# Two heads at a time in the last eight attention steps of block 2's last mixer

## What is computed

```python
def odd_mixer(hn, w_in, qn, kn, w_out):
    z = (hn @ w_in).reshape(B, S, 3, 16, 64)
    q, k, v = rms_norm(z[:, :, 0], qn), rms_norm(z[:, :, 1], kn), z[:, :, 2]
    o = moba_attention(q, k, v, alibi_slopes(16), 64 ** -0.5)
    return o.reshape(B, S, 1024) @ w_out
# 256 tokens are one block of keys, so moba_attention is causal attention:
#   scores = q k^T - slope * distance, masked; softmax; times v
```

## Time and profile before

| | us |
|---|---|
| median of three runs | 1979.36 |
| lowest, highest | 1979.27, 1981.42 |
| the profiled execution itself | 1981.44 |
| its span | 1979.70 |

### The profile page before, as it was taken

The page is one execution under the profiler, slowest core; times in us unless marked ns, Lnnn a source line. Parts: engine busy times, 40 slices in busy tenths (PEclk is TensorE's granted clock), DMA queues, the critical chain, the costliest instruction groups (busy, mean ns, idle before and its releaser), DMA issues.

```text
span 1979.7 us, 24390 instructions
## 1 busy us (share of the span) xinstructions
PE 1946.0 (98%) x9160; PEld 1594.2 (81%) x9160; DVE 1211.2 (61%) x1506; ACT 919.5 (46%) x1143; POOL 85.0 (4%) x161
## 2 busy tenths in 40 slices
PE   9999999999999999999999999899999999999999
PEld 7888888887888788788878888786788887778887
DVE  5555776677446644667668555676555466765545
ACT  5443435545443444343653544366444355644433
POOL 2000100000000100000000000000000000000000
PEclk9999999999999999999999999998999999999999
DMA  9575653446554855564445655453365555336542
GB/s 311 189 220 177 214 189 130 168 149 213 191 191 149 270 190 185 191 219 160 140 169 167 216 184 184 135 173 124 118 239 170 170 180 182 107 123 233 171 168 86
DMA packets 201325, 353.51 MB, mean 179 GB/s; under 512 B 7985, under 2 KB 101089, under 8 KB 201249
## 3 DMA queue, kind: packets, MB, share of 16 engines
q1 hardware_dynamic: 195856, 334.85, 50.7%
q0 software_dynamic: 5392, 17.62, 2.9%
HBM read 351.39 MB, written 1.05 MB: 178 GB/s over the span
## 4 chain that ended last, share of the span: by engine, by line
PE 85%; DVE 5%; issue 5%; DVEq 2%; ACT 2%; DMA 0%; POOL 0%; SPq 0%; ACTq 0%; POOLq 0%
PE acc L686 48%; PE aux L686 29%; DVE w_low L2050 1%; PE aux L802 1%; PE aux L701 1%; PE aux L956 1%; ACT w_high L1492 1%; DVE x_res L2136 1%; PE aux L1250 1%; DVE xT_low L2056 0%; PE aux L1249 0%; DVEq L2102 0%; PE aux L1270 0%; PE aux L1258 0%; DMA w_raw<-ffn_w 0%
## 5 line engine op out<-in xcount | busy, mean ns | idle before, releaser
L2050 DVE TENSOR_TENSOR w_low<-w_raw,w_high 128x2048 fp32r<-128x2048 f32 (+2 forms) x308 | 695.5, 2271 | 425.8 <-ACT w_high L1492 423.3
L1492 ACT CAST w_high<-w_raw 128x2048 fp32r<-128x2048 f32 (+1 forms) x312 | 587.6, 1898 | 431.2 <-PE acc L686 323.9
L686 PE MATMUL aux<-w_high,xT_high 128*128 128x512 f32 x960 | 380.8, 397 | 3.5 <-DVE xT_low L2056 1.7
L686 PE MATMUL aux<-w_high,xT_low 128*128 128x512 f32 x960 | 374.7, 390 | 0.0
L686 PE MATMUL aux<-w_low,xT_high 128*128 128x512 f32 x960 | 373.8, 389 | 0.0
L686 PE MATMUL acc<-w_high,yT_high 128*128 128x512 f32 (+1 forms) x836 | 330.9, 396 | 2.4 <-DVE yT_low L2202 2.3
L686 PE MATMUL acc<-w_high,yT_low 128*128 128x512 f32 (+1 forms) x836 | 326.0, 390 | 0.0
L686 PE MATMUL acc<-w_low,yT_high 128*128 128x512 f32 (+1 forms) x836 | 325.8, 390 | 0.0
L686 PE MATMUL acc<-w_high,xT_high 128*128 128x512 f32 (+2 forms) x752 | 297.4, 395 | 5.7 <-DVE xT_low L2056 4.1
L686 PE MATMUL acc<-w_high,xT_low 128*128 128x512 f32 (+2 forms) x752 | 291.5, 388 | 0.0
L686 PE MATMUL acc<-w_low,xT_high 128*128 128x512 f32 (+2 forms) x752 | 291.2, 387 | 0.0
(11 more groups left out here) (307 smaller groups left out, 1356.5 us busy)
## 6 DMA issues: line engine op xcount, KB each, us to landing
w_raw<-ffn_w SPq DMA_DIRECT2D x174, 512.0 KB
w_raw<-w_ff SPq DMA_DIRECT2D x64, 1024.0 KB
w_raw<-w_in SPq DMA_DIRECT2D x52, 1024.0 KB
w_raw<-ffn_w SPq DMA_DIRECT2D x44, 1024.0 KB
w_raw<-w_branch SPq DMA_DIRECT2D x16, 1024.0 KB
w_raw<-o_w_in SPq DMA_DIRECT2D x12, 1024.0 KB
w_raw<-w_ple_gate SPq DMA_DIRECT2D x8, 1024.0 KB
w_raw<-e_w_in SPq DMA_DIRECT2D x6, 1024.0 KB
```

Source lines behind the costliest of these rows:

```text
L686: last = nc.tensor.matmul(dst, lhs[:, kt, tok], rhs(j), start=(kt == k_first and q == 0), stop=(kt == k_last and q == 2))
L1492: nc.scalar.copy(whi[:, s, 0:size], raw[:, s, 0:size]).then_inc(slot_hi[s], 1)
L2050: V.tensor_tensor(wlo[:, s, 0:size], raw[:, s, 0:size], cast(whi[:, s, 0:size]), ALU.subtract)\
```

## The change

The steps of heads 0 to 7 stay as they are, but for the values of head 6, which move out of step 7, and for two jobs of ScalarE in step 7 that change places (the copy of head 7 now comes ahead of the copy of z5). Heads 8 to 15 are done in four iterations g = 4 to 7 of two heads. TensorE's order in one: values of pair g-1, scores of heads 2g+2 and 2g+3, six products, transposes of 2g, three products, transposes of 2g+1, three products (in g = 4 the six products come first). The last pair's values stand in `out_end`.

- `score_pair` interleaves two heads: both short matmuls, then both long ones. The heads lie on different row halves. It waits until both banks are read.
- `values_pair` interleaves two heads on the two column halves of `woven_o`.
- ScalarE's order in an iteration: copy of pair g-1, copies of heads 2g and 2g+1, exponentials of 2g+2 and 2g+3, a high unit in g = 4, 5 and 6.
- VectorE keeps its order head by head; only the low part of a pair moves, from odd steps to even ones (from h = 8 on, pair h/2-1 ahead of the scores of h+2).
- There are four buffers of probabilities in place of three; the turned probabilities of odd heads go to another buffer.

The same products are computed, from the same weight units.

```diff
@@ -370,18 +370,18 @@
-            return stat_[:, :, :].rearrange("p a b -> p (a b)")[:, 2 * (h % 3) + t:2 * (h % 3) + t + 1]
+            return stat_[:, :, :].rearrange("p a b -> p (a b)")[:, 2 * (h % 4) + t:2 * (h % 4) + t + 1]
...
-            return stat_[:, :, :].rearrange("p a b -> p (a b)")[:, 2 * (h % 3):2 * (h % 3) + 2]
+            return stat_[:, :, :].rearrange("p a b -> p (a b)")[:, 2 * (h % 4):2 * (h % 4) + 2]
...
         def probs(h):
-            return flat(bk)[:, (h % 3) * 3 * P:(h % 3 + 1) * 3 * P]
+            return flat(bk)[:, (h % 4) * 3 * P:(h % 4 + 1) * 3 * P]
...
         def probs_T(h):
-            return flat(bk)[:, (3 + h % 2) * 3 * P:(4 + h % 2) * 3 * P]
+            return aT if h % 2 else flat(bk)[:, 4 * 3 * P:5 * 3 * P]
@@ -1195,7 +1195,7 @@
             quad2("c", xTh, xTl, tile1=norm_T1, tile1_at=(1, 0))
-            def piece(name, j, t):
+            def piece(name, j, t, ks=range(4)):
@@ -1205,9 +1205,9 @@
                 vh, vl = (w[:, s, :].rearrange("p (k n) -> p k n", k=4) for w in (whi, wlo))
-                last = products(acc[:, p, t, :], [(4 * j + k, k) for k in range(4)], 0, KT - 1, xTh, xTl, t,
+                last = products(acc[:, p, t, :], [(4 * j + k, k) for k in ks], 0, KT - 1, xTh, xTl, t,
                                 lambda k: vh[:, k, :], lambda k: vl[:, k, :])
-                if (j, t) == (1, 1):
+                if (j, t, ks[-1]) == (1, 1, 3):
                     last.then_inc(acc_full[p], 1)
@@ -1238,6 +1238,19 @@
+            def score_pair(n0, h, q, k, late=()):
+                if h >= 2:
+                    pe.wait_ge(s_ready, DEPTH * H1 + n0 + h)
+                for name in late:
+                    p, n = JOB[name]["acc"][0]
+                    pe.wait_ge(acc_read[p], acc_n2(p, n) + 2)
+                for i in (h, h + 1):
+                    nc.tensor.matmul(woven_score(i)[:, 0:P], q(i, 0, P), k(i, 0, P), start=True, stop=True)
+                for i in (h, h + 1):
+                    nc.tensor.matmul(woven_score(i)[:, P:3 * P], q(i, P, S), k(i, 0, S), start=True, stop=True)\
+                        .then_inc(score_full, 1)
             def score(n0, h, q, k, late=()):
@@ -1258,6 +1271,19 @@
                 at_T[n0 + h] = n_aux[2].k + 1
+            def values_pair(n0, g, v):
+                pe.wait_ge(aux_read[2], at_T[n0 + 2 * g + 1])
+                if g > 0:
+                    pe.wait_ge(o_read, n0 // 2 + g)
+                heads = [(woven_o[i * HD:(i + 1) * HD, :], probs_T(i), v(2 * g + i)) for i in range(2)]
+                for o, p, (v0, v1) in heads:
+                    nc.tensor.matmul(o[:, 0:P], v0, p[:, 0:P], start=True, stop=True)
+                for o, p, (v0, v1) in heads:
+                    nc.tensor.matmul(o[:, P:S], v0, p[:, P:2 * P], start=True, stop=False)
+                for o, p, (v0, v1) in heads:
+                    nc.tensor.matmul(o[:, P:S], v1, p[:, 2 * P:3 * P], start=False, stop=True).then_inc(o_full, 1)
@@ -1387,6 +1413,10 @@
+            def odd_scores(h):
+                score_pair(ODD0, h, lambda h, c0, c1: half(flat(bv), h, c0, c1),
+                           lambda h, c0, c1: half(kT_odd, h, c0, c1))
             def odd_v(h):
@@ -1401,8 +1431,8 @@
             odd_score(1)
-            for h in range(MOBA_H):
-                if h + 2 < MOBA_H and h not in (0, 6):
+            for h in range(8):
+                if h not in (0, 6):
                     odd_score(h + 2)
@@ -1425,28 +1455,42 @@
                     odd_score(8)
-                elif h == 7:
+                else:
                     piece("z5", 1, 1)
-                elif h == 8:
+                probs_turned(ODD0, h)
+                if 0 < h < 7:
+                    values(ODD0, h - 1, odd_v)
+            for g in range(4, MOBA_H // 2):
+                if g == 4:
                     out_piece("oout", 0, 0, (0, 1))
-                elif h == 9:
-                    out_piece("oout", 1, 0, (0, 1))
-                elif h == 10:
-                    out_piece("oout", 0, 0, (2, 3))
-                elif h == 11:
+                values_pair(ODD0, g - 1, odd_v)
+                if 2 * g + 2 < MOBA_H:
+                    odd_scores(2 * g + 2)
+                if g == 5:
+                    out_piece("oout", 0, 1, (0, 1))
+                elif g == 6:
                     out_piece("oout", 1, 0, (2, 3))
-                elif h == 12:
-                    out_piece("oout", 0, 1, (0, 1))
-                elif h == 13:
-                    out_piece("oout", 0, 1, (2, 3)).then_inc(unit_used, 1)
-                elif h == 14:
+                elif g == 7:
                     out_piece("oout", 2, 0, (0, 1))
+                probs_turned(ODD0, 2 * g)
+                if g == 4:
+                    out_piece("oout", 1, 0, (0,))
+                elif g == 5:
+                    out_piece("oout", 0, 0, (2,))
+                elif g == 6:
+                    out_piece("oout", 0, 1, (2,))
                 else:
-                    out_piece("oout", 3, 0, (0, 1))
-                probs_turned(ODD0, h)
-                if h > 0:
-                    values(ODD0, h - 1, odd_v)
-            out_end("oout", lambda: values(ODD0, MOBA_H - 1, odd_v))
+                    out_piece("oout", 3, 0, (0,))
+                probs_turned(ODD0, 2 * g + 1)
+                if g == 4:
+                    out_piece("oout", 1, 0, (1,))
+                elif g == 5:
+                    out_piece("oout", 0, 0, (3,))
+                elif g == 6:
+                    out_piece("oout", 0, 1, (3,)).then_inc(unit_used, 1)
+                else:
+                    out_piece("oout", 3, 0, (1,))
+            out_end("oout", lambda: values_pair(ODD0, MOBA_H // 2 - 1, odd_v))
             ff_and_side(1)
@@ -1952,7 +1996,7 @@
                 nc.scalar.copy(probs_T(h), aux[:, 2, 0:3 * P]).then_inc(aux_read[2], 1)
-                if h % 2 == 0 and h > 0:
+                if h % 2 == 0 and h > 0 and n0 == 0:
                     pair_copy(n0, h // 2 - 1)
@@ -2008,11 +2052,10 @@
             head_exps(ODD0, 1, 1.0)
-            for h in range(MOBA_H):
+            for h in range(MOBA_H // 2):
                 if h == 6:
                     copy_T("kt1", kT_odd[:, D:2 * D], 2)
-                if h + 2 < MOBA_H:
-                    head_exps(ODD0, h + 2, 1.0)
+                head_exps(ODD0, h + 2, 1.0)
                 if h == 1:
@@ -2021,17 +2064,26 @@
                     nc.scalar.copy(two(buf[:, D:2 * D]), acc[:, 0]).then_inc(acc_read[0], 1)
-                elif h == 7:
+                head_copies(ODD0, h)
+                if h % 2 == 0 and h > 0:
+                    pair_copy(ODD0, h // 2 - 1)
+                if h == 7:
                     full("z5")
                     to_sbuf("z5", bval[:, :, NC:D])
-                head_copies(ODD0, h)
                 if h < 3:
...
                     high_unit(unit0 + 8 + h)
-                elif h in (8, 9):
-                    high_unit(unit0 + h + 6)
-                elif h == 13:
+            for g in range(4, MOBA_H // 2):
+                pair_copy(ODD0, g - 1)
+                head_copies(ODD0, 2 * g)
+                head_copies(ODD0, 2 * g + 1)
+                for h in (2 * g + 2, 2 * g + 3):
+                    if h < MOBA_H:
+                        head_exps(ODD0, h, 1.0)
+                if g in (4, 5):
+                    high_unit(unit0 + 10 + g)
+                elif g == 6:
                     split_unit("oout", 0)
@@ -2893,8 +2945,10 @@
             for h in range(MOBA_H):
-                if h % 2 and h > 1:
+                if h in (3, 5, 7):
                     pair_low((h - 3) // 2)
+                elif h % 2 == 0 and h > 7:
+                    pair_low(h // 2 - 1)
                 if h + 2 < MOBA_H:
...
```

## The result

Over 20 executions each, the changed kernel takes 1983.51 us in the median (1979.21 to 1986.37) and the kernel before 1979.65 us (1977.51 to 1984.56). The ratio, an estimate from the executions of both kernels (it is not the quotient of the medians, which lie 3.86 us apart), is 1.0014 with a 95% interval of 1.0008 to 1.0020: 2.8 us slower, 1.6 to 4.0. The forecast was 1981.2 us, slower by 1.85, and a range of 1977.5 to 1986.5. One of the 12 executions of experiment e1 took 2159.01 us at a mean granted clock of 0.85 and is left out of its ratio. The profiled execution took 1983.08 us with a span of 1981.3 us, against 1981.44 and 1979.7: 1.6 us more.

The account below looks back on a forecast made before the run. TensorE, busy 98%, was taken to bound the kernel; 6.8 us leave it, but 9.5 us of waits on a VectorE and ScalarE loop come (0.8 were there): 1979.36 + 1.85 = 1981.2 us, range 1977.5 to 1986.5.

Parts of the forecast that it names:

- the walk: Three engine queues followed in written order from head 7's transposes: 9.5 us of waits come, last values 1.8 us later.
- TensorE's own queue: Heads 8 to 15: scores in pairs 2.5, values in pairs 4.0, products in quarters 0.3, together 6.8 us less.
- rival C: Value pairs: column halves do not overlap, 1.46 us a pair, 3.2 us slower in all, 1982.5 us; chance 0.10.
- The loop: VectorE and ScalarE jobs from probabilities(2g+1) round to the next probabilities set the pace, 8.8 us a pair, no TensorE job.
- Weight loads at nothing: Low units 14 and 15 end 1.9 and 3.5 us later, delaying DMA slots; hidden products cover it, priced at nothing.
- Sum: Whole execution: median shown 1979.36 plus 1.85 gives 1981.2 us.
- the likeliest case: Queue walk without a paid clock fall: 1981.2 us, own range 1980.5 to 1982.2, chance 0.40.
- the part above 1983.3: Slower than 1983.3 us: two thirds of the clock rival and part of the no-overlap rival, chance 0.28.
- rival A: Clock falls in TensorE's new waits: 1.85 plus 1 to 5.1 us, 1982.2 to 1986.3, middle 1984; chance 0.33.
- The sign named for A: Clock row of 1720 to 1765 in the profile after would read 0.9 and less instead of 1.00.
- Rival B: Other engines keep up and TensorE bounds again: 1971.8 us, or 1976.5 with waits cut to half; chance 0.17.

Follow-up runs that it names:

- e1: Changed kernel with ScalarE's copies of pairs 4, 5, 6 ahead of the high units; head 7 to last values 27.72 us, ratio to before 0.9985.
- e3: Changed kernel with ScalarE's and VectorE's orders both edited and the low unit moved one place; stretch 24.37 us twice, ratios to before 0.9959 and 0.9978.
- e4: Changed kernel with pairs kept but each head's matmuls issued together instead of interleaved; stretch 32.43 us, ratio to before 1.0017.
- e2: Changed kernel with VectorE's probabilities of head 2g+1 ahead of the pair's low part and next scores; stretch 25.30 us, ratio to before 0.9979.
- e5: Changed kernel with 29 extra unused products put in front of TensorE's late waits; stretch 32.17 us, ratio to before 1.0012.
- c0: The changed kernel run again without edit, as yardstick; stretch 32.17 us, ratio to before 1.0006.

## Why the prediction was right

Point by point, with the walk's times less 0.06 us (the stretch began so much earlier in this trace):

| step | forecast | measured |
|---|---|---|
| first value pair (6/7) | 1722.50 | 1722.40 |
| transposes 9, wait | 1726.30, 0.95 | 1726.25, 0.95 |
| transposes 11, wait | 1733.57, 1.8 | 1733.56, 1.81 |
| scores 14, wait | 1736.91, 1.3 | 1736.82, 1.25 |
| transposes 13, wait | 1742.34, 2.0 | 1742.29, 1.94 |
| transposes 14, wait | 0.6 | none |
| transposes 15, wait | 1749.95, 2.5 | 1749.88, 1.44 |
| last values | 1752.51 | 1752.39 |

- **TensorE's own queue, 6.8 us less.** In the stretch it was busy 29.69 us before and 22.85 in e3, both at a clock of 1.00: 6.84 less. (The 6.6 us of the page is a difference of whole spans, with stretches of low clock in both.) The value pair, which no row showed, was put at 0.80 us and took 0.81. The Trainium skill's page "TensorE: Matmul & The Clock Gate" (Part 3) puts column packing within some 5 ns of row packing. This trace agrees where the heads are interleaved: 0.81 us for two heads against 0.80 for one on columns, 0.86 against 0.85 on rows. Where a head's matmuls are issued together, in e4, the two differ (values 1.07 us, scores 0.87). So rival C fell. That both column halves write one bank cost nothing in the interleaved order.
- **The loop, 8.8 us a pair.** 8.73 us in the trace. e1 and e2 cut it at two different places and each gained what the walk said for its place, to 0.2 us; e5 shows that TensorE's work is not in it.
- **Weight loads at nothing.** Behind the last values both traces take 229 us, so no load came late enough to cost time.
- **Sum.** 1.85 us forecast, 1.71 in the stretch, 1.6 in the spans of the profiled executions; the ratios of the two sets stand for 2.8 and 1.2 us, with intervals that hold 1.71. The waits listed in the walk add up to 9.2 us, not 9.5; the rest is the 0.3 us ahead of the first value pair, which the walk's times contain and the trace shows (0.29).
- **How good a hit it was.** The mechanism and the stretch were hit; the median less so. 1983.51 us lies above the likeliest case's own range (1980.5 to 1982.2), in the part above 1983.3 that was given 0.28, and near the middle of rival A's prices (1984), although A is not what happened. The forecast of 1981.2 us is 2.3 below that median, of which 0.3 is the kernel before itself (1979.65 in place of 1979.36). What is more than the stretch's 1.71 us in the medians (3.86 and 2.37 apart) no trace shows; executions of one kernel scatter by more than that.
- **Rival A, the clock.** Its premise came true and its price did not. After the wait of 1.94 us the granted clock was 0.53 for 3.6 us, nearly all of it at the lower of the two levels (1.2 GHz), here in the windows view of the changed kernel:

```profile
1743.20:1746.80 3.60, 3.60 (x19) 2.64 (x18) 2.84 (x7) 2.28 (x10) 0.00 (x0) 0.53 0.02 5
```

The slow stretch made TensorE arrive at transposes 14 when their probabilities were there, and took 1 us off the wait of transposes 15 (1.44 in place of 2.5): it was absorbed, as the rival itself had said of a fall before 1746. These are the two lines of the table above that differ, and they moved nothing behind them.

The trace of the changed kernel alone could be read the other way. TensorE is busy 24.50 us of its stretch, 1.65 more than the 22.85 of the same work in e3 at full clock, and the waits are 7.7 us in place of the 9.5 forecast; one could take the slow 1.65 us for the loss of 1.71. e5 decides between the two readings: its clock is 1.00 over the whole stretch, transposes 14 wait 0.44 us (0.6 forecast), and the stretch takes the same 32.17 us. Whether some execution pays for a fall behind the last long wait is not shown; no trace here had one. The sign named for A, 0.9 and less over 1720 to 1765, was too coarse: the row of 1720 to 1760 reads 0.96.
- **Rival B** was to decide from where the waits sum to under 7.6 us. The 7.7 us measured come close to that, but by the slow stretch and not by faster engines: at full clock they were forecast at 9.5, and 32.17 less TensorE's 22.85 is 9.3. e1 and e2, at full clock, brought them down to 4.4 and 2.3 us (the 0.29 of the first value pair counted), and with that each was faster than before.

## What to carry to other kernels

When work is taken off the busiest engine, walk the other engines' queues in their written order with durations from the timeline, also where they look half idle: here VectorE was busy 61% and ScalarE 46% of the span (75% and 58% of the stretch before the change: 22.70 and 17.64 of 30.46 us), and a loop through the two of them still set the pace. In such a loop look for long jobs with loose deadlines (weight casts) ahead of short ones with tight deadlines (a pair's copy, a head's probabilities), and for results wanted in this iteration that stand behind inputs of the next; reordering them cost nothing and turned +1.7 us into -6.1. Follow a job that is moved until the queue is empty, or its wait turns up one step on. And when a wait looks as if the clock had caused it, fill it with work and see whether the time moves.

## What the runs showed that was not expected

- An independent head on the other column half overlaps fully when interleaved (0.81 us for two), partly when issued behind (1.07); on the row halves the order made no difference (0.86 and 0.87).
- The scatter of whole executions goes with the mean granted clock. Of the 27 executions of the kernel before that ran beside c0 (1977.99 to 1984.82 us), the ten with a mean clock of 0.997 took 1979.8 us on average and the six with 0.995 took 1982.4. One place where the traces differ in the clock is the first mixer of block 2, which no edit touched. These are the windows rows of 1330 to 1420 of c0 and of e3, same columns as above:

```profile
1330.00:1420.00 90.00, 84.55 (x434) 64.58 (x433) 58.06 (x172) 50.22 (x117) 2.63 (x6) 0.94 0.28 93
```

```profile
1330.00:1420.00 90.00, 82.89 (x446) 63.53 (x444) 60.52 (x174) 50.28 (x118) 4.77 (x8) 1.00 0.29 94
```

With the clock at 0.94 of full in the one and 1.00 in the other, the transposes of head 7 came at 1721.71 and 1718.44 us of the span. Comparing within a trace took this out. Both traces of e3 read 1.00 there and the other eight 0.94, so it is not shown that this is chance from one execution to the next; why the clock fell in one and not in the other stays open.
